# Two blocks with a 16-expert layer on one core: one expert load divided unevenly over the partitions, and idle TensorE products in the last expert

## What is computed

```
cap = max(1, EC_CAPACITY_FACTOR * n // N_EXPERTS)             # 32
gate, idx = lax.top_k(jnp.swapaxes(aff, 1, 2), cap)
xs = jax.vmap(lambda hb, ib: hb[ib])(h, idx)                  # (16, 32, 1024)
a = jnp.einsum('becd,edf->becf', xs, w_gate)                  # w_gate: 16 x 1024 x 2048
u = jnp.einsum('becd,edf->becf', xs, w_up)                    # w_up:   16 x 1024 x 2048
y = jnp.einsum('becf,efd->becd', jax.nn.silu(a) * u, w_down) * gate[..., None].astype(h.dtype)
```

## Time and profile before

| | us |
|---|---|
| median of 3 runs | 1540.61 |
| the profiled execution's own time | 1540.27 |
| its span, first to last instruction | 1538.5 |
| TensorE busy (share of the span) | 1204.2 (78%) |
| VectorE busy | 615.3 (40%) |
| ScalarE busy | 429.7 (28%) |
| DMA queue of SP: 541.08 MB, share of 16 engines | 85.1% |

### The profile page before, as it was taken

One profiled execution on the slowest core, in us unless ns is written; L12 is line 12 of the kernel. 1 busy time (PEld: TensorE's weight loads), 2 busy tenths in 40 slices (PEclk: granted clock), 3 DMA queues, 4 the chain that ended last, 5 costly groups with the idle time before them and its releaser, 6 DMA issues.

```text
span 1538.5 us, 18557 instructions
## 1 busy us (share of the span) xinstructions
PE 1204.2 (78%) x7530; PEld 698.6 (45%) x7530; DVE 615.3 (40%) x1048; ACT 429.7 (28%) x652; POOL 35.5 (2%) x60
## 2 busy tenths in 40 slices
PE   9999999999999999987666566566565665665665
PEld 7888877887888899622111111111111111111112
DVE  5687789888777867511011011011011011011111
ACT  4665367786564664300000000000000000000001
POOL 0100000010001000000000000000000000000000
PEclk9999999999999999988777677877877777777788
DMA  9876876675755566999999999999999999999996
GB/s 384 323 271 229 299 269 245 227 284 197 284 183 199 219 239 274 409 435 429 433 430 430 433 431 429 432 432 429 429 436 428 429 436 426 432 435 425 434 434 281
DMA packets 40277, 550.12 MB, mean 358 GB/s; under 512 B 5001, under 2 KB 5289, under 8 KB 10497
## 3 DMA queue, kind: packets, MB, share of 16 engines
q1 hardware_dynamic: 37328, 541.08, 85.1%
q0 software_dynamic: 2576, 7.56, 1.5%
q10 hardware_dynamic: 288, 0.30, 0.1%
HBM read 547.84 MB, written 1.61 MB: 357 GB/s over the span
## 4 chain that ended last, share of the span: by engine, by line
PE 47%; DMA 34%; DVE 11%; ACT 3%; issue 3%; DVEq 0%; SPq 0%; ACTq 0%; POOL 0%
PE ps L671 45%; DMA b<-in_w_down 34%; DVE b L1636 5%; PE ps L675 3%; ACT b L1255 2%; DVE b L1653 2%; DVE b L2382 1%; DVE b L2323 1%; ACT b L1257 1%; DMA b<-in_dense 1%; DVE b L2329 1%; DVE b L2361 0%; DVE b L2363 0%; DVE b L1667 0%; ACT L1255 0%
## 5 line engine op out<-in xcount | busy, mean ns | idle before, releaser
L671 PE MATMUL ps<-b,b 128*32 128x512 f32 (+6 forms) x7070 | 1134.1, 536 | 288.0 <-DMA b<-in_w_up 113.3
L671 PEld LDWEIGHTS ps<-b,b 128*32 128x32 f32 (+2 forms) x7070 | 640.8, 158 | 742.5 <-issue 447.7
L1255 ACT ACTIVATE b<-ps 128x512 f32<-128x512 f32 (+4 forms) x169 | 93.4, 553 | 870.6 <-PE ps L671 571.8
L1636 DVE TENSOR_TENSOR b<-b,b 128x1024 fp32r<-128x1024 f32 (+5 forms) x254 | 277.1, 1091 | 95.2 <-ACT b L1255 76.8
L1255 ACT ACTIVATE b<-b 128x1024 fp32r<-128x1024 f32 (+6 forms) x219 | 219.1, 1000 | 191.7 <-PE ps L671 171.6
L2372 DVE TENSOR_TENSOR b<-b,ps 128x512 f32<-128x512 f32 x16 | 11.0, 689 | 391.4 <-issue 378.2
L2382 DVE TENSOR_TENSOR b<-b,ps 128x1024 f32<-128x1024 f32 x28 | 34.2, 1222 | 301.8 <-PE ps L671 301.8
L675 PE MATMUL ps<-b,b 128*128 128x128 f32 (+1 forms) x360 | 70.1, 322 | 37.3 <-DVE b L1667 22.9
L675 PEld LDWEIGHTS ps<-b,b 128*128 128x128 f32 (+1 forms) x360 | 45.8, 168 | 87.6 <-DVE b L1667 36.1
L1653 DVE SCALAR_TENSOR_TENSOR b<-b,b,b 128x512 f32<-128x512 f32 (+3 forms) x50 | 63.2, 1264 | 4.3 <-ACT b L1255 0.5
L1636 DVE TENSOR_TENSOR b<-ps,b 128x512 f32<-128x512 f32 (+8 forms) x73 | 38.3, 524 | 33.1 <-PE ps L671 14.3
(11 more groups left out here) (62 smaller groups left out, 204.2 us busy)
## 6 DMA issues: line engine op xcount, KB each, us to landing
b<-in_w_up SPq DMA_DIRECT2D x29, 4096.0 KB, 43.1
b<-in_w_down SPq DMA_DIRECT2D x29, 4096.0 KB, 38.3
b<-in_w_gate SPq DMA_DIRECT2D x28, 4096.0 KB, 42.9
b<-in_dense SPq DMA_DIRECT2D x88, 1024.0 KB, 5.3
b<-in_w_ada SPq DMA_DIRECT2D x24, 1024.0 KB, 6.9
b<-in_w_gate SPq DMA_DIRECT2D x6, 2048.0 KB, 10.1
b<-in_w_down SPq DMA_DIRECT2D x5, 2048.0 KB, 9.9
b<-in_ada SPq DMA_DIRECT2D x8, 1024.0 KB, 19.0
```

The source lines that it names most:

```text
L671: return e.matmul(o, lhsT, rhs, start=start, stop=stop, skip_group_check=True)
L1255: e.activation(o, i, f, bias=bias, scale=scale).then_inc(mark[0], 1)
L1636: e.tensor_tensor(o, a, b, op).then_inc(mark[0], 1)
```

## The change

It has two parts.

**An uneven load.** The first down pair of expert 8 (`E_UNEVEN = 8`, pair number 45, buffer 0) is no longer one DMA. Columns 0 to 6655 still go to all 128 partitions in one DMA. The last 1536 columns of partitions 0 to 63 are loaded in eight DMAs of 8 partitions (each fourth partition of a block of 32). The same columns of partitions 64 to 127 go, by 16 further DMAs, not to their own partitions but 64 lower, into two buffers of their own (`HIGH2`, 512 columns, and `HIGH3`, 1024 columns). The bytes are the same, in 25 DMAs in place of one; 384 KB of them are written to partitions 0 to 63 that were written to 64 to 127 before. TensorE therefore computes three of expert 8's down products in two halves of 64 rows (`down_uneven`), and two more flips and one more copy by ScalarE bring the upper rows' operand to the lower partitions (`HTX`).

**Idle products.** In the last expert TensorE gets 8 idle products before the wait for chunk 4, 8 before that for chunk 6, 6 before that for `HD`, and 4 before that for chunk 10.

```diff
+E_UNEVEN = 8
+E_UNEVEN_PAIR = (E_UNEVEN * 12 + 8 - E_FIRST) // 2
+E_UNEVEN_PARTS = 25
...
+        HIGH3, HIGH2, HTX = buf(HT_AT + 12, D), at(104, W), at(111, 2, P)
...
-            return EP[i][:, g * 4096:(g + 1) * 4096], (S(f"ew{i}"), 16 * (m // E_PAIRS + 2 + (i in E_TWICE)))
+            return EP[i][:, g * 4096:(g + 1) * 4096], (S(f"ew{i}"), 16 * (m // E_PAIRS + 2 + (i in E_TWICE) + (E_UNEVEN_PARTS - 1) * (m >= E_UNEVEN_PAIR and i == E_UNEVEN_PAIR % E_PAIRS)))
...
+            def uneven_pair(to, src, landed_):
+                e.dma_start(to[:, 0:6656], src[:, 0:6656]).then_inc(landed_, 16)
+                for i in (0, 1, 2, 3, 32, 33, 34, 35):
+                    low, high = slice(i, i + 32, 4), slice(64 + i, min(64 + i + 32, P), 4)
+                    e.dma_start(to[low, 6656:8192], src[low, 6656:8192]).then_inc(landed_, 16)
+                    e.dma_start(HIGH2[low, :], src[high, 6656:7168]).then_inc(landed_, 16)
+                    e.dma_start(HIGH3[low, :], src[high, 7168:8192]).then_inc(landed_, 16)
...
-                if m < pairs - 1:
+                if m == E_UNEVEN_PAIR:
+                    uneven_pair(EP[i], pair_src(n), S(f"ew{i}"))
+                elif m < pairs - 1:
                     e.dma_start(EP[i], pair_src(n)).then_inc(S(f"ew{i}"), 16)
...
+            def down_uneven(w, b, nd, o):
+                high = HIGH3[0:64, nd * W:(nd + 1) * W] if b == 3 else HIGH2[0:64, :]
+                mm(o, HTT[0:64, b, 32:64], w[0:64, b * D + nd * W:b * D + (nd + 1) * W], False, False)
+                return mm(o, HTX[0:64, b - 2, 32:64], high, False, False)
...
+                    if x == NE - 1 and c in (4, 6):
+                        keep_clock(8, 7)
                     e.wait_ge(*expert_weight(n)[1])
...
+                if x == NE - 1:
+                    keep_clock(6, 7)
                 e.wait_ge(S("v_hd"), x + 1)
                 if x:
-                    e.wait_ge(S("a_ht"), x)
+                    e.wait_ge(S("a_ht"), x + (x > E_UNEVEN))
+                if x == E_UNEVEN:
+                    for b in (2, 3):
+                        flip(ps[0:64, 2, (b - 2) * P:(b - 1) * P], HD[:, 256 + b::4])
...
-                e.wait_ge(S("a_ht"), x + 1)
+                e.wait_ge(S("a_ht"), x + 1 + (x >= E_UNEVEN))
...
+                    if x == NE - 1 and c == 10:
+                        keep_clock(4, 7)
...
+                            elif (x, c) == (E_UNEVEN, 9) and 2 * b + nd >= 5:
+                                ins = down_uneven(w, b, nd, ps[32 * g:32 * g + 32, 5, :])
...
+                if x == E_UNEVEN:
+                    copy(HTX.rearrange("p a b -> p (a b)")[0:64, :], ps[0:64, 2, 0:T], to=S("a_ht"))
                 copy(HTT.rearrange("p a b -> p (a b)"), ps[:, 4, :], to=S("a_ht"))
```

## The result

The changed kernel took **1542.69 us** (median of 21 runs, 1542.04 to 1543.83), the kernel before 1540.39 beside it (21 runs, 1540.17 to 1541.19): a ratio of 1.0014 with a 95% interval of 1.0008 to 1.0020. It is slower by 2.3 us; the interval is 1.2 to 3.1. The forecast was 1539.4 in a range that ended at 1541.3. The profiled execution took 1542.13 us with a span of 1540.3, 1.8 longer than that of before.

A forecast was written before the change was run, and what follows sets the result against it. The prediction took the DMA stream of loads, with uneven engines at its end, to bound the kernel. Terms of -1.3 and +0.1 gave -1.2 us: 1539.1 profiled, 1539.4 as median, range 1538.5 to 1541.3.

The forecast's parts named there:

- What bounds the kernel: Expert stage: DMA engines never pause at 431 GB/s, so lags stay; about 3.6 us of the end are imbalance.
- The failed step: End of the load: the late engines write upper partitions, are spared 1.8 us and end at 1525.9.
- The straggler: Engine running dry around 1524.3; taken as lower, it ends at 1526.1 to 1526.6 and sets the load's end, 1.3 us earlier.
- The shares: Share of DMA engines busy per microsecond after 1521 us, 0.59 falling to 0.01; read as about seven or eight late engines.
- the second rival: Late engines aren't the upper eight: one late lower engine gets 2.3 us more, kernel slower at 1542.9; chance 0.12.
- A set of about eight late ones beside about eight others looks like a half: Argument from the count of engines working after 1521 us that the late ones are the upper eight.
- The price: Expert 8's uneven load: each lower engine gets 2.3 us more, bounds 1.8 and 4.3, from bytes at the small-piece rate.
- SP and the queue: Expert 8: SP issues 24 more DMAs, could be held once by 16.6 us; 25 us stay queued, so no cost.
- The idle products: Last expert's TensorE: extra products raise the clock, 0.65 us gained against 0.75 late, 0.1 lost.
- the forecast's doubt: Last expert, chunks 6 and 7: 4.0 us idle before them leaves them partly slow, 5.3 us taken where 3.64 is fastest.
- The rule that the rival named: Skill's rule that engines 7 and 15 are usually slow; the first writes lower partitions, so the move would end slower.
- the two terms: Load's end 1.3 us earlier by the uneven load, and 0.1 us lost by the idle products in the last expert.

The follow-up runs named there:

- spare_all: Kernel before, with the last 1536 columns of the expert-8 pair not loaded for any partition; 1538.71 us against 1540.65.
- after_probe: Changed kernel plus one tiny load of 8 partitions behind the last parts, for which GpSimd waits; 1543.42 us.
- before_probe: Kernel before plus one tiny load of 8 partitions behind the last parts, for which GpSimd waits; 1540.65 us for 1540.60.
- extra_lower: Kernel before, with the upper rows' 1536 columns loaded a second time to spare places on lower partitions; 1542.71 us against 1540.65.
- uneven_512: Changed kernel without idle products, moving 512 columns in place of 1536, in 17 transfers; 1542.44 us against 1540.76 for the kernel before.
- uneven_only: Changed kernel without its four groups of idle products; 1543.11 us against 1540.60 for the kernel before.
- idle_only: Kernel before with the four groups of idle products alone, no uneven load; 1541.02 us against 1540.60.
- probe16: Kernel before plus sixteen tiny loads of 1 to 16 partitions behind the last parts, GpSimd waiting for each in turn; 1540.77 us for 1540.36.

## Why the prediction was wrong

**What bounds the kernel: right.** The end hangs on the stream, no engine makes up for a lag, and a lag has the same worth at expert 8 as at the end: `spare_all` spared 1.82 us there and got 1.94 (0.5 to 3.1) at the end.

**The failed step** is "If the late engines are the upper ones, they end at 1527.7 - 1.8 = 1525.9", with what follows from it, "The straggler then decides". The shares gave the number of late engines, seven or eight, and the step read a place from it for all of them. The rest of the step came true: in `after_probe` the last of the upper engines ends at 1525.8, the lower ones that were dry end at 1523.0 to 1523.8 (forecast 1523.6), and the straggler at 1526.0 (1526.1 to 1526.6). But two of the eight late engines were lower. They ended at 1527.7 to 1527.9 in `before_probe` and end at 1529.6 and 1529.9 in `after_probe`, and they decide, not the straggler. With a late lower engine the end moves by what a lower engine is given, and the saving of the upper eight buys nothing. That is the second rival as it was worked out: 1542.9 against the measured 1542.69. It had 0.12, and the range stopped short of it. What spoke against it, "A set of about eight late ones beside about eight others looks like a half", was true of six of the eight. The end goes by the last engine, so that wasn't enough.

**The price: right.** 2.3 us more for a lower engine (between 1.8 and 4.3); the probes differ by 2.14, and `extra_lower` lost 2.06. That it is made up of bytes at the rate of small pieces, as the sum has it, is not shown (`uneven_512`).

**SP and the queue: right**, and cheaper than bounded, 2.83 us held in place of 16.6. The products in halves and the extra copy can't be told from nothing at the end: `extra_lower`, without them, loses 2.06, `uneven_only` 2.5.

**The idle products: right in the sum.** Forecast 0.1 lost; `idle_only` gives 0.4 lost, between 0.9 gained and 1.7 lost, and `uneven_only` is no faster than the whole change. The clock was better than forecast: 3.64 us for chunks 6 and 7 in place of 5.3. Before chunk 6 TensorE was idle for 2.36 us, as the timeline has it, and not 4.0. In `idle_only` the same pair took 6.53 us after a wait of 4.05, so the forecast's doubt was fair. What was missing is that it would not matter: once the load comes later, the gain turns into a wait for chunk 8 of 1.53 us.

**The rule that the rival named**, engines 7 and 15 as the slow ones (the Trainium skill, DMA: Bandwidth & Descriptors, "Latency and other measured facts"), gave the right sign by the wrong engine: here the waits of `probe16` place late ones at 5 and 6, and none of 7 to 15 holds a wait up longer. The Trainium skill itself ties that row to transfers issued by GpSimd, and these loads are issued by SyncE, so the rule did not bear on this case.

What the two terms gave: forecast -1.3 and +0.1, measured +2.5 (`uneven_only`) and +0.4 not told from nothing.

## What to carry to other kernels

How many are late doesn't tell who. Before work is moved from one half of a set of engines to the other, find the last one by name: a row of tiny transfers of 1 to 16 partitions behind the last load costs one run and no time that could be told (0.4 us, interval from 1.2 less to 1.8 more), the trace's counts of the last load's semaphore say how many engines end when, and a pair of one-sided edits (spare the one half, load the other) tells what each half is worth. Where work goes to a side with a single engine that is last, the saving of all others is worth nothing. A gain that needs an unread fact should keep the other reading's time in its range.

## What the runs showed of the hardware

- **Fetches of instructions make single DMA engines late, and for good.** While the loads bind, each packet of 16 KB put one of eight engines back by about 1.6 us, though it took 1.0 us itself (0.3% x 16 x 1541 us / 74). Seven engines got none of it, and no lag shrank in 800 us. Fourteen packets more (74 for 60) cost 2.9 us (1.5 to 4.3), though the products they belong to lay in waits.
- **The rate of a load goes with the partitions that it takes.** 112 neighbouring partitions of 32 KB rows with two groups of 8 behind them moved 121 to 269 GB/s for 30 us (1095 to 1125), and 16 partitions, each eighth one, went down to 237; 8 partitions, each fourth one, beside a whole load kept 422 to 435. What makes the difference is not shown.
- **Many transfers hold the queue that issues them:** 43 held SP for 37.3 us, 25 for 19 (1063.05 to 1082.1).
